# Attention weights transposed by a product with the diagonal of inverse denominators, in a pipeline one pair deeper, without the spreading products

## The chip, the cores and the metric

One core of a Trainium2 chip runs the whole kernel. The metric is the device time of one execution in microseconds (us), as a median over runs. "A product" below is one matrix product on TensorE (PE); in fp32 it leaves two records in the trace, a PE transpose leaves one.

## The reference

The kernel computes one step of a two-layer backbone on 128 context and 512 latent tokens (model width 1024). Each layer has adaLN-modulated RMSNorm, one input projection, three parallel head groups, an output projection and a SwiGLU FFN. The head group that matters here is the attention:

```python
def softmax_with_sink(s, sink):
    sk = sink.astype(jnp.float32).reshape(N_KV_HEADS, Q_PER_KV, 1, 1)
    m = jnp.maximum(jnp.max(s, axis=-1, keepdims=True), sk)
    e = jnp.exp(s - m)
    return e / (jnp.sum(e, axis=-1, keepdims=True) + jnp.exp(sk - m))

    # latent_attention: queries in blocks of 128, keys of the block before, the same and the next one
    s_lat = jnp.einsum('bnqkgd,bnskd->bnkgqs', qb, kband) * ATTN_SCALE
    s_ctx = jnp.einsum('bnqkgd,bckd->bnkgqc', qb, k_ctx.astype(jnp.float32)) * ATTN_SCALE
    s_lat = jnp.where(mask[None, :, None, None], s_lat, NEG)
    p = softmax_with_sink(jnp.concatenate([s_lat, s_ctx], axis=-1), sink)
    o = (jnp.einsum('bnkgqs,bnskd->bnqkgd', p[..., :3 * BLOCK], vband)
         + jnp.einsum('bnkgqc,bckd->bnqkgd', p[..., 3 * BLOCK:], v_ctx.astype(jnp.float32)))
```

There are 8 query heads and 2 key/value heads of 64 channels. The other two groups are RWKV-7 mixing (a chunked recurrence) and a Fourier transform; they and the FFN are not changed.

## The kernel before

Each engine has its own instruction stream, written by hand in one block per engine: `tensor` (PE), `scalar` (ACT), `vector` (DVE), `gpsimd` (POOL), `sync`. Semaphores order them; there is no scheduler, so each engine works strictly in the order of its stream. A layer runs: input projection, low-rank and Fourier products, attention stage A, two groups of the recurrence, attention stage B, three groups of the recurrence, output projection, FFN. So there are four attention stages in an execution.

A stage works through "pairs" m = (query block b, head j); a pair holds the two heads g = 0, 1 of the two key/value groups, one above the other in the 128 partitions. Stage A has 8 pairs (blocks 0 and 1), stage B 12 (blocks 2, 3 and the context block 4). Block 0 and 3 read 3 key tiles of 128, blocks 1 and 2 read 4, block 4 reads 1. For each pair:

- S, `scores(m)` on PE (the products of line 1332): queries times keys into PSUM, into two banks used in turn;
- softmax, `softmax_in(m)` on DVE: line 2447 writes the sink column, line 2449 adds the mask, takes the maximum and writes the scores into `Pm` (3 buffers) for each g;
- exp, `pexp(m)` on ACT (line 1940): exponentials in place and their sum into `den`;
- T, `transposes(m)` on PE (line 1355): each 128x128 tile of `Pm` through a PE transpose into PSUM bank 4 or 5 (one for each g, a single buffer);
- `ptcopy(m)` on ACT (line 1951): PSUM to `PT`;
- inverse, `inverse(m)` on DVE: reciprocal of `den` (line 2456), then `dg` = identity times 1/den, 128x2x128 (line 2459);
- V, `values(m)` on PE (line 1370): values times `PT`, summed over the key tiles, into columns 0 to 127 of bank 6 or 7; then the spreading products (line 1374), ones times `dg`, which put 1/den of each query into all rows of columns 128 to 255;
- `normalise(m)` on DVE: a copy of the spread inverses (line 2469), then the multiplication of the output with them (line 2470), into `qt`.

In iteration m of the loop PE does S(m), T(m-1), V(m-2); ACT does exp(m), ptcopy(m-1); DVE does softmax(m), normalise(m-3), inverse(m-1) and, in some iterations, a piece of other work (`between`). When the last S is done PE also transposes the first tiles of the next recurrence group (`token_tiles`, lines 1319 to 1322), and after the last V it runs that group's `products`. T(m) waits for exp(m) and for `pt_sb`, ptcopy of the pair before.

Ahead of stage A PE does `lora_rows("w", 1)`, a column step, `ada_rows(10)`, `lora_rows("a", 1)` (lines 977, 978), and then `ft1` (line 1242), and ACT does the matching `lora_sigmoid` (lines 1828, 1829) and row copies (line 1801). PE's step for ft1 needs the PSUM bank that the sigmoid of ("a", 1) reads.

Of the kernel before, what the change touches and what calls it, by code (L numbers as in the profile page):

```python
# [280 lines left out]
def build(nc, I, O):  # L281
# [5 lines left out]
    MUL, ADD, SUB, MAX = ALU.mult, ALU.add, ALU.subtract, ALU.max  # L287
    ctx = ExitStack()
    with ctx:
# [640 lines left out]
        def _(e):  # L930
# [33 lines left out]
            for l in range(DEPTH):  # L964
# [81 lines left out]
                def ada_cols(j, la):  # L1046

                    e.wait_ge(mrow_sb.sem, mrow_sb.upto(la, j + 1))
                    bank, at = (ps[4], 8 * ADA_BLOCK[j]) if j < 4 else (ps[5], 8 * j)
                    last = mm(bank[:, at:at + 8], mrow[:, :],  # L1050
                              ident.rearrange("p (g s) -> p g s", g=4)[:, :, 0:2], start=True, stop=True)
                    last.then_inc(mcol_ps(), 1)
# [212 lines left out]

                lora_rows("w", 1)
                ada_cols(9, l)
                ada_rows(10, l)
                lora_rows("a", 1)
                taken(e, l, ("fn", 0))  # L1270
                taken(e, l, ("fn", 1))
                e.wait_ge(ld_dft.sem, ld_dft.upto(l, ld_dft.per))
# [64 lines left out]
                def attention(first, last_pair, items_before, scored, then):  # L1337

                    def scores(m):
                        if m - 2 < first:  # L1340
                            q_ = (m + 1) % 2
                            e.wait_ge(acc_free[q_].sem, acc_free[q_].upto(l, (items_before + 1 - q_) // 2))
                        else:
                            e.wait_ge(s_sb.sem, s_sb.upto(l, 2 * (m - 1)))
                        score_products(m)

                    def transposes(m):
                        b, j = ATT[m]
                        for g in range(2):
                            n = 2 * m + g  # L1350
                            e.wait_ge(p_exp.sem, p_exp.upto(l, n + 1))
                            if n >= 2:
                                e.wait_ge(pt_sb.sem, pt_sb.upto(l, n - 1))
                            for c in range(len(key_tiles(b))):
                                last = tr(ps[4 + g][:, 128 * c:128 * c + 128], Pm[:, m % 3, g, 1 + 128 * c:129 + 128 * c],  # L1355
                                          ident)
                            last.then_inc(pt_ps(), 1)

                    def values(m):
                        b, j = ATT[m]  # L1360
                        bank = ps[6 + m % 2]
                        if m >= 2:
                            e.wait_ge(o_sb.sem, o_sb.upto(l, m - 1))
                        e.wait_ge(pt_sb.sem, pt_sb.upto(l, 2 * m + 2))
                        tiles = key_tiles(b)
                        for c, (kind, t) in enumerate(tiles):
                            for g in range(2):
                                v = (ckv[:, 1, 64 * g:64 * g + 64] if kind == "cache"
                                     else vtok[:, 128 * t + 64 * g:128 * t + 64 * g + 64])
                                mm(bank[64 * g:64 * g + 64, 0:128], v, PT[:, m % 4, c, g, :],  # L1370
                                   start=(c == 0), stop=(c == len(tiles) - 1))
                        e.wait_ge(den_diag.sem, den_diag.upto(l, m + 1))
                        for g in range(2):
                            last = mm(bank[64 * g:64 * g + 64, 128:256], ones[:, :], dg[:, m % 2, g, :],
                                      start=True, stop=True)
                        last.then_inc(pv_done(), 1)

                    for m in range(first, last_pair + 2):
                        if m < last_pair and m >= first + scored:
                            scores(m)  # L1380
                        if first <= m - 1 < last_pair:
                            transposes(m - 1)
                        if m == last_pair:
                            ready_for(then)
                            e.wait_ge(s_sb.sem, s_sb.upto(l, 2 * last_pair))
                            for n in range(2):
                                token_tiles(then, n)
                        if first <= m - 2 < last_pair:
                            values(m - 2)
                    for n in range(2):  # L1390
                        products(then, n)

# [327 lines left out]
        def _(e):  # L1720
# [36 lines left out]
            for l in range(DEPTH):  # L1757
# [40 lines left out]
                def ada_rows(j, la):  # L1798
                    e.wait_ge(ada_done.sem, ada_done.upto(la, 2 * j + 2))
                    e.wait_ge(mcol_ps.sem, mcol_ps.upto(la, j))  # L1800
                    act(mrow[:, :], ps[6 + j % 2][:, 0:128], ACT.Copy).then_inc(mrow_sb(), 1)
# [114 lines left out]
                act(kcT[:, :], cx[:, 256:384], ACT.Copy).then_inc(free(), 1)  # L1916
                ada_rows(9, l)
                lora_sigmoid("w", 1)
                ada_rows(10, l)
                lora_sigmoid("a", 1)  # L1920
                act(exp_table[:, :], eps[:, 0:1], ACT.Exp)
                ft1_copy(0)
                ft1_copy(1)
# [9 lines left out]
                def attention(first, last_pair):  # L1933

                    def pexp(m):
                        b, j = ATT[m]
                        w = 128 * len(key_tiles(b)) + 1
                        for g in range(2):
                            e.wait_ge(s_sb.sem, s_sb.upto(l, 2 * m + g + 1))
                            act(Pm[:, m % 3, g, 0:w], Pm[:, m % 3, g, 0:w], ACT.Exp, scale=-1.0,  # L1940
                                bias=negm[:, b % 2, j, g:g + 1],
                                accum_out=den[:, b % 2, j, g:g + 1]).then_inc(p_exp(), 1)

                    def ptcopy(m):
                        b, j = ATT[m]
                        nt = len(key_tiles(b))
                        if m >= 4:
                            e.wait_ge(pv_done.sem, pv_done.upto(l, m - 3))
                        for g in range(2):
                            e.wait_ge(pt_ps.sem, pt_ps.upto(l, 2 * m + g + 1))  # L1950
                            act(PT[:, m % 4, 0:nt, g, :], ps[4 + g][:, 0:128 * nt].rearrange("p (c t) -> p c t", c=nt),
                                ACT.Copy).then_inc(pt_sb(), 1)

                    for m in range(first, last_pair + 1):
                        if m < last_pair:
                            pexp(m)
                        if first <= m - 1 < last_pair:
                            ptcopy(m - 1)

                attention(0, NATT_A)  # L1960

# [232 lines left out]
        def _(e):  # L2194
# [77 lines left out]
            for l in range(DEPTH):  # L2272
# [165 lines left out]
                def attention(first, last_pair, between):  # L2438
# [14 lines left out]
                    def inverse(m):  # L2453
                        b, j = ATT[m]
                        e.wait_ge(p_exp.sem, p_exp.upto(l, 2 * m + 2))
                        own.after(V.reciprocal(den[:, b % 2, j, :], den[:, b % 2, j, :]))
                        if m >= 2:
                            e.wait_ge(pv_done.sem, pv_done.upto(l, m - 1))
                        V.tensor_tensor(dg[:, m % 2, :, :], ident.unsqueeze(1).to_broadcast([128, 2, 128]),
                                        den[:, b % 2, j, :].unsqueeze(2).to_broadcast([128, 2, 128]),  # L2460
                                        MUL).then_inc(den_diag(), 1)

                    def normalise(m):
                        b, j = ATT[m]
                        bank = ps[6 + m % 2]
                        e.wait_ge(pv_done.sem, pv_done.upto(l, m + 1))
                        if m >= 2:
                            e.wait_ge(o_sb.sem, o_sb.upto(l, m - 1))
                        own.after(V.tensor_copy(inv_row[:, m % 2, :], bank[:, 128:256]))
                        V.tensor_tensor(qt[:, j, 128 * b:128 * b + 128], bank[:, 0:128], inv_row[:, m % 2, :], MUL).then_inc(o_sb(), 1)  # L2470

                    for m in range(first, last_pair + 3):
                        if m < last_pair:
                            softmax_in(m)
                        if first <= m - 3 < last_pair:
                            normalise(m - 3)
                        if first <= m - 1 < last_pair:
                            inverse(m - 1)
                        if m - first in between:
                            kind, step = between[m - first]  # L2480
                            kind(step)
# [422 lines left out]
```

## Time and profile before

| what | us |
|---|---|
| median of 3 runs | 1833.74 (1831.01 to 1835.14) |
| the profiled execution | 1831.18 |
| its span, first to last instruction | 1829.2 |
| PE busy | 1741.3 (95%) |
| DVE busy | 1064.0 (58%) |
| ACT busy | 803.5 (44%) |
| mean granted TensorE clock | 0.994 |

Time in a trace counts from the first instruction. A timeline row is a run of instructions of one line on one engine: its start, its length, what it writes and reads, how many records; a bracket tells how long the engine sat idle before it and what ended that. Records on PE overlap (one lasts about 0.27 us, the next begins after 0.05 to 0.22 us), so costs on PE are read from start to start.

### The profile page before, as it was taken

What the parts mean: (1) busy time and instruction counts of PE and PEld (TensorE: products, weight loads), DVE (VectorE), ACT (ScalarE), POOL (GpSimd) and SP (SyncE); (2) the same over time, 40 slices, a digit from 0 to 9 for tenths busy, and PEclk for the clock granted to TensorE, in tenths of its full rate; (3) what the DMA queues carried; (4) which work ended last, traced back from release to release, by engine and by line L of the source; (5) the groups of instructions that cost most, each with busy time, mean ns of one, the idle gap of its engine ahead of it and who ended that gap; (6) DMA issues with size and microseconds to landing.
All of it is one profiled execution on the core that took longest, in us unless ns stands there. A gap on an engine that the chain in (4) does not pass through costs nothing. (4 is left out here: it accounts for less than half of the span.)

```text
span 1829.2 us, 46190 instructions
## 1 busy us (share of the span) xinstructions
PE 1741.3 (95%) x19693; PEld 1629.1 (89%) x19693; DVE 1064.0 (58%) x2328; ACT 803.5 (44%) x1729; POOL 370.7 (20%) x306
## 2 busy tenths in 40 slices
PE   7999988889999999999999999888999999999997
PEld 5999776779899999999989987677898999999997
DVE  4535767663494673838453556675619647365663
ACT  3343655552453351535443356465326525344352
POOL 3254010212302003020324431002231120201112
PEclk9999999999999999999999999999999999999999
DMA  9654600004613313241327362000021232323211
GB/s 335 212 128 143 170 5 3 4 6 130 172 58 88 86 60 102 59 114 53 99 88 202 92 195 64 4 3 7 25 70 51 65 107 68 104 61 90 84 56 58
DMA packets 215973, 161.11 MB, mean 88 GB/s; under 512 B 21968, under 2 KB 213146, under 8 KB 215770
## 3 DMA queue, kind: packets, MB, share of 16 engines
q1 hardware_dynamic: 213818, 156.13, 29.0%
q8 instruction: 157, 2.57, 0.6%
q0 software_dynamic: 1952, 2.03, 0.4%
q14 instruction: 46, 0.38, 0.1%
HBM read 154.99 MB, written 3.15 MB: 86 GB/s over the span
## 5 line engine op out<-in xcount | busy, mean ns | idle before, releaser
L2674 DVE SCALAR_TENSOR_TENSOR x<-PS,mod,x 128x320 f32<-128x320 f32 (+2 forms) x240 | 90.8, 434 | 289.3 <-PE PS L1082 289.3
L1118 PE MATMUL PS<-T_hi,wsplit 128*128 128x320 f32 x768 | 170.0, 309 | 0.0
L822 POOL TENSOR_TENSOR SfR<-ring,SfR 128x768 fp32r<-128x768 f32 (+1 forms) x24 | 41.2, 1715 | 582.3 <-ACT SfR L1790 582.3
L1081 PE MATMUL PS<-in_hi,win 128*128 128x320 f32 x480 | 149.9, 320 | 0.7 <-POOL win L822 0.7
L1082 PE MATMUL PS<-in_hi,win 128*128 128x320 f32 x480 | 144.6, 309 | 0.0
L1081 PE MATMUL PS<-hid_hi,wsplit 128*128 128x320 f32 x440 | 133.1, 310 | 0.0
L1082 PE MATMUL PS<-hid_hi,wsplit 128*128 128x320 f32 x440 | 132.5, 309 | 0.0
L1118 PEld LDWEIGHTS PS<-T_hi,wsplit 128*128 128x128 f32 x768 | 128.3, 188 | 0.0
L1118 PE MATMUL PS<-h_hi,wsplit 128*128 128x320 f32 x576 | 127.6, 309 | 0.0
L1118 PE MATMUL PS<-T_lo,wsplit 128*128 128x320 f32 x384 | 118.7, 309 | 0.0
L2107 ACT ACTIVATE wsplit<-Sf 128x512 fp32r<-128x512 f32 x96 | 59.8, 629 | 130.0 <-DVE Sf L2724 72.3
L2744 DVE TENSOR_TENSOR E<-E,PS 128x320 f32<-128x320 f32 x120 | 58.6, 488 | 87.4 <-PE PS L1118 87.1
L822 POOL TENSOR_TENSOR win<-ring,win 128x1024 fp32r<-128x1024 f32 x30 | 72.5, 2416 | 161.6 <-ACT win L1790 161.4
L1790 ACT ACTIVATE win<-ring 128x1024 fp32r<-128x1024 f32 x30 | 31.8, 1061 | 153.7 <-PE PS L1082 130.0
L822 POOL TENSOR_TENSOR wsplit<-ring,wsplit 128x768 fp32r<-128x768 f32 (+2 forms) x42 | 74.3, 1775 | 119.4 <-ACT wsplit L1790 119.4
L1118 PEld LDWEIGHTS PS<-h_hi,wsplit 128*128 128x128 f32 x576 | 96.3, 188 | 0.0
L1081 PEld LDWEIGHTS PS<-in_hi,win 128*128 128x128 f32 x480 | 90.0, 188 | 4.8 <-issue 4.2
L1082 PEld LDWEIGHTS PS<-in_hi,win 128*128 128x128 f32 x480 | 90.2, 188 | 1.9 <-issue 1.9
L1118 PE MATMUL PS<-h_lo,wsplit 128*128 128x320 f32 x288 | 89.0, 309 | 0.0
L886 POOL TENSOR_TENSOR mix<-mix,eye 128x128 f32<-128x128 f32 x40 | 16.5, 413 | 343.6 <-DVE mix L2521 343.6
L1081 PEld LDWEIGHTS PS<-hid_hi,wsplit 128*128 128x128 f32 x440 | 82.6, 188 | 0.5 <-issue 0.5
L1082 PEld LDWEIGHTS PS<-hid_hi,wsplit 128*128 128x128 f32 x440 | 82.6, 188 | 0.0
(539 smaller groups left out, 5399.4 us busy)
## 6 DMA issues: line engine op xcount, KB each, us to landing
ring<-in_w_ada SPq DMA_DIRECT2D x47, 1024.0 KB, 6.8
ring<-in_ffn_w_in SPq DMA_DIRECT2D x88, 512.0 KB, 5.1
ring<-in_ffn_w_out SPq DMA_DIRECT2D x16, 768.0 KB, 4.4
ring<-in_ffn_w_out SPq DMA_DIRECT2D x16, 640.0 KB, 4.0
ring<-in_w_in SPq DMA_DIRECT2D x7, 1024.0 KB, 9.6
ring<-in_w_in SPq DMA_DIRECT2D x10, 512.0 KB, 5.6
ring<-in_w_in SPq DMA_DIRECT2D x16, 256.0 KB, 5.6
ring<-in_w_out SPq DMA_DIRECT2D x16, 256.0 KB, 8.1
```

Source lines behind the costliest of these rows:

```text
L822: nc.gpsimd.tensor_tensor(lo, raw_w, hi, SUB).then_inc(wl_ready(), 1)
L886: nc.gpsimd.tensor_tensor(E1D[p], LP[p][:, :, BA, :], eye64[:, :].unsqueeze(1).to_broadcast([128, 2, 64]), ADD).then_inc(diag_sb(), 1)
L1081: mm(lat[:, 0:TH], w, v[:, 0:TH], start=(n == 0), stop=(n == total - 1))
L1082: last = mm(cx[:, 0:TH], w, v[:, TH:T], start=(n == 0), stop=(n == total - 1))
L1118: last = mm(bank[:, 0:TH], (w_lo if p == 1 else w_hi)[:, k, :], (v_lo if p == 2 else v_hi)[:, k, :], start=(q in (A11, A12, S1_) and k == ...
L1790: act(hi, raw_w, ACT.Copy).then_inc(wh_ready(), 1)
L2107: act(hi, raw_b, ACT.Copy).then_inc(bh_ready(), 1)
L2674: last = V.scalar_tensor_tensor(x[:, m, a:b], bank[:, at:at + b - a], mod[:, gate_at + m, s:s + 1], x[:, m, a:b], MUL, ADD)
L2744: V.tensor_tensor(v, v, bank[:, 0:TH], op).then_inc(ps_taken(), 1)
```

## The change

Four edits, in all three compute engines:

1. T multiplies each tile of `Pm` by `dg[:, m % 2, g, :]` in place of transposing it through the identity: the result is the transposed tile with each query's column already divided by its denominator. T waits for `den_diag` (the inverse of the pair) in place of `p_exp`.
2. The two spreading products of V are left out, and normalise is one copy of the output.
3. The pipeline is one pair deeper: in iteration m PE does S(m), T(m-2), V(m-3); ACT exp(m), ptcopy(m-2); DVE softmax(m), inverse(m-1), normalise(m-4). The token tiles now stand ahead of T(last-1). Each loop has one iteration more. `dg` is free for reuse once T has read it.
4. `lora_rows("a", 1)` on PE and `lora_sigmoid("a", 1)` on ACT stand ahead of `ada_rows(10)`.

```diff
@@ PE, ahead of the Fourier transform
                 lora_rows("w", 1)
                 ada_cols(9, l)
+                lora_rows("a", 1)
                 ada_rows(10, l)
-                lora_rows("a", 1)
@@ PE, attention
                     def transposes(m):
                         b, j = ATT[m]
+                        e.wait_ge(den_diag.sem, den_diag.upto(l, m + 1))
                         for g in range(2):
                             n = 2 * m + g
-                            e.wait_ge(p_exp.sem, p_exp.upto(l, n + 1))
                             if n >= 2:
                                 e.wait_ge(pt_sb.sem, pt_sb.upto(l, n - 1))
                             for c in range(len(key_tiles(b))):
-                                last = tr(ps[4 + g][:, 128 * c:128 * c + 128], Pm[:, m % 3, g, 1 + 128 * c:129 + 128 * c],
-                                          ident)
+                                last = mm(ps[4 + g][:, 128 * c:128 * c + 128], Pm[:, m % 3, g, 1 + 128 * c:129 + 128 * c],
+                                          dg[:, m % 2, g, :], start=True, stop=True)
                             last.then_inc(pt_ps(), 1)
@@ PE, values(m)
-                                mm(bank[64 * g:64 * g + 64, 0:128], v, PT[:, m % 4, c, g, :],
-                                   start=(c == 0), stop=(c == len(tiles) - 1))
-                        e.wait_ge(den_diag.sem, den_diag.upto(l, m + 1))
-                        for g in range(2):
-                            last = mm(bank[64 * g:64 * g + 64, 128:256], ones[:, :], dg[:, m % 2, g, :],
-                                      start=True, stop=True)
+                                last = mm(bank[64 * g:64 * g + 64, 0:128], v, PT[:, m % 4, c, g, :],
+                                          start=(c == 0), stop=(c == len(tiles) - 1))
                         last.then_inc(pv_done(), 1)
 
-                    for m in range(first, last_pair + 2):
+                    for m in range(first, last_pair + 3):
                         if m < last_pair and m >= first + scored:
                             scores(m)
-                        if first <= m - 1 < last_pair:
-                            transposes(m - 1)
                         if m == last_pair:
                             ready_for(then)
                             e.wait_ge(s_sb.sem, s_sb.upto(l, 2 * last_pair))
                             for n in range(2):
                                 token_tiles(then, n)
                         if first <= m - 2 < last_pair:
-                            values(m - 2)
+                            transposes(m - 2)
+                        if first <= m - 3 < last_pair:
+                            values(m - 3)
@@ ACT
                 lora_sigmoid("w", 1)
+                lora_sigmoid("a", 1)
                 ada_rows(10, l)
-                lora_sigmoid("a", 1)
@@ ACT, attention
-                    for m in range(first, last_pair + 1):
+                    for m in range(first, last_pair + 2):
                         if m < last_pair:
                             pexp(m)
-                        if first <= m - 1 < last_pair:
-                            ptcopy(m - 1)
+                        if first <= m - 2 < last_pair:
+                            ptcopy(m - 2)
@@ DVE, inverse(m) and normalise(m)
                         if m >= 2:
-                            e.wait_ge(pv_done.sem, pv_done.upto(l, m - 1))
+                            e.wait_ge(pt_ps.sem, pt_ps.upto(l, 2 * (m - 1)))
@@
-                        own.after(V.tensor_copy(inv_row[:, m % 2, :], bank[:, 128:256]))
-                        V.tensor_tensor(qt[:, j, 128 * b:128 * b + 128], bank[:, 0:128], inv_row[:, m % 2, :], MUL).then_inc(o_sb(), 1)
-
-                    for m in range(first, last_pair + 3):
+                        V.tensor_copy(qt[:, j, 128 * b:128 * b + 128], bank[:, 0:128]).then_inc(o_sb(), 1)
+
+                    for m in range(first, last_pair + 4):
                         if m < last_pair:
                             softmax_in(m)
-                        if first <= m - 3 < last_pair:
-                            normalise(m - 3)
                         if first <= m - 1 < last_pair:
                             inverse(m - 1)
+                        if first <= m - 4 < last_pair:
+                            normalise(m - 4)
```

## Rows read from the trace of the kernel before

**Rows 1.** The page: busy time of engines, share, instructions.

```profile
PE 1741.3 (95%) x19693; PEld 1629.1 (89%) x19693; DVE 1064.0 (58%) x2328; ACT 803.5 (44%) x1729; POOL 370.7 (20%) x306
```

**Rows 2.** First stages A and B: stretch, length, busy PE, PEld, DVE, ACT, POOL, clock, DMA.

```profile
210.76:238.51 27.75, 25.46 (x273) 20.00 (x272) 20.39 (x74) 21.55 (x57) 0.00 (x0) 1.00 0.20 66
292.52:326.50 33.98, 31.13 (x328) 23.26 (x328) 27.99 (x112) 24.29 (x75) 0.00 (x0) 1.00 0.01 2
```

**Rows 3.** Timeline of PE in the first stage A: start, length, line, tiles, records.

```profile
218.27 0.88 PE L1355 MATMUL PS<-mats,mix 128*128 128x128 f32 x6
219.08 0.66 PE L1370 MATMUL PS<-mix 128*64 128x128 f32 x8
219.57 0.39 PE L1370 MATMUL PS<-mix,ckv 128*64 128x128 f32 x4
219.79 0.39 PE L1374 MATMUL PS<-mix,ones 128*64 128x128 f32 x4
220.10 0.92 PE L1332 MATMUL PS<-mix 64*128 64x384 f32 x4
...
221.17 0.88 PE L1355 MATMUL PS<-mats,mix 128*128 128x128 f32 x6
...
231.06 1.09 PE L1355 MATMUL PS<-mats,mix 128*128 128x128 f32 x8
232.08 0.88 PE L1370 MATMUL PS<-mix 128*64 128x128 f32 x12
```

**Rows 4.** PE's lines 1355 and 1374 in the whole execution (ns min/median/max).

```profile
L1355 PE MATMUL PS<-mats,mix x240: 272/273/331, 213.3 to 1216.0; 128*128 128x128 f32 x120
L1374 PE MATMUL PS<-mix,ones x160: 270/271/273, 217.1 to 1218.1; 128*64 128x128 f32 x160
```

**Rows 5.** Timeline of PE: single fp32 products of 128x128, last steps before stage A.

```profile
210.10 0.38 PE L1262 MATMUL PS<-mix 128*128 128x128 f32 x2
210.32 0.39 PE L1263 MATMUL PS<-mix 128*128 128x128 f32 x2
210.54 0.29 PE L1050 MATMUL PS<-mats,mrow 128*128 128x8 f32 x2
```

**Rows 6.** The weight loads of line 1262 (ns min/median/max).

```profile
L1262 PEld LDWEIGHTS PS<-mix x8: 187/188/188, 205.6 to 1102.7; 128*128 128x128 f32 x8
```

**Rows 7.** PE's waits in the first stages A and B (us, times, longest).

```profile
PE PS L1355 <- ACT mix L1951: 1.4, 3, 0.9
PE PS L1355 <- ACT mix L1940: 0.7, 1, 0.7
...
PE PS L1355 <- ACT mix L1951: 1.8, 5, 0.6
PE PS L1355 <- ACT mix L1940: 1.0, 1, 1.0
```

**Rows 8.** Timeline of DVE at the opening of stage A.

```profile
214.30 0.43 DVE L2459 TENSOR_TENSOR mix<-mats,den 128x256 f32<-128x256 f32 x1
```

**Rows 9.** Timeline of DVE and PE at the opening of stage B, and at its fifth pair.

```profile
296.79 0.43 DVE L2459 TENSOR_TENSOR mix<-mats,den 128x256 f32<-128x256 f32 x1
...
303.82 0.49 PE L1332 MATMUL PS<-kcT,mix 64*128 64x128 f32 x4
```

**Rows 10.** Timeline of ACT and PE ahead of stage A: the low-rank and Fourier steps.

```profile
194.39 0.28 ACT L1801 ACTIVATE mrow<-PS 128x128 f32<-128x128 f32 x1 [0.46 <-PE PS L1041]
...
192.37 1.95 PE L1041 MATMUL PS<-ring,csil 128*32 128x128 f32 x64
194.25 1.14 PE L977 MATMUL PS<-mix,lora 64*128 64x512 f32 x4
...
196.84 0.67 PE L1242 MATMUL PS<-mix 128*128 128x256 f32 x2 [1.23 <-ACT mix L1829]
```

**Rows 11.** Timeline of DVE: normalise of one pair.

```profile
219.61 0.29 DVE L2469 COPY mix<-PS 128x128 f32<-128x128 f32 x1
...
220.15 0.15 DVE L2456 RECIPROCAL den<-den 128x2 f32<-128x2 f32 x1
```

## The prediction

> **What bounds the kernel now.** The first view to read is the busy time of the engines: PE is busy for 1741.3 of 1829.2 us, DVE for 1064.0, ACT for 803.5 [rows 1]. That says that PE bounds most of the execution, not that it bounds the attention, so I read the four attention stages by themselves. In the first layer they last 27.75 and 33.98 us, of which PE is busy for 25.46 and 31.13, 5.1 us of idle time in all; the second-busiest engine of stage A, ACT, has 21.55 of 27.75, and that of stage B, DVE, 27.99 of 33.98 [rows 2]. The second layer runs the same code on the same shapes, so one stage A and one stage B carry the argument, and each counts twice. The clock granted in both is 1.00, the 2.4 GHz level.
>
> Then PE's timeline, from start to start. For a pair of 3 key tiles T takes 219.08 - 218.27 = 0.81 us, V 219.79 - 219.08 = 0.71, the spreading products 220.10 - 219.79 = 0.31, and S of the following pair, with 4 tiles, 221.17 - 220.10 = 1.07 [rows 3]. Start follows start there with no idle time, so in the middle of a stage PE sets the pace. What idle time there is stands at the opening, where the first T waits for the first exponentials, and in front of some T, which wait for ACT's copy (line 1951) of the pair before: 0.7 + 1.4 us in stage A and 1.0 + 1.8 in stage B are named [rows 7]. The stages thus hold work to be added to (PE's) and some 5 us a layer of named waits that could take it up.
>
> **The transposing products.** A T of 3 tiles has 6 records in 0.81 us, one of 4 tiles 8 records in 232.08 - 231.06 = 1.02 [rows 3]. Two more records make 0.21, so a transpose costs 0.11 us and each T a fixed 0.15 or so (0.81 - 6 x 0.11). There are 240 of them in the execution [rows 4]. What replaces each is a full fp32 product, 128 rows, 128 stationary and 128 moving columns, with a new stationary tile each time. The trace has that form in lines 1262 and 1263: 210.32 - 210.10 = 0.22 and 210.54 - 210.32 = 0.22 us [rows 5]. Its two weight loads last 0.188 us each [rows 6], and 0.22 is less than two of them, so they lie beside the products. Added: 240 x (0.22 - 0.11) = +26.4 us of PE work. The form is the same, but at most two stand in a row there, with six or eight to come; the bounds are 0.11 (no dearer than the transpose) and 0.376 (both weight loads bare, 2 x 0.188). I take 0.22, because it is the same shape on the same engine.
>
> The row shows a product at twice the price of a transpose. The Trainium skill, "TensorE: Matmul & The Clock Gate", section Terms, says that transpose mode is 4 times faster for FP32, and "Perfetto Trace Analysis", section Transposes, asks that a logical transpose be done as a transpose and not as a matmul. By the first the price would be 4 x 0.11 = 0.44 and the term 240 x 0.33 = +79 us; by the rows it is +26.4. The second speaks against this edit, and the rows agree with its direction.
>
> **The spreading products.** Of the 0.31 us between 219.79 and the next S about 0.09 is the gap that follows V in any case: the four records before them, of the same form, take only 219.79 - 219.57 = 0.22 [rows 3]. There are 160 records, four for each of 40 pairs [rows 4]: 40 x 0.22 = -8.8 us. On DVE normalise lasts from 219.61 to 220.15, 0.54 us, and becomes one copy of about 0.25 [rows 11]: -0.3 us a pair on an engine that PE's work covers. Worth nothing, unless DVE is what T waits for.
>
> PE's work so grows by 26.4 - 8.8 = +17.6 us, or for stage A (56 products, 8 pairs) 6.2 - 1.8 = +4.4, for stage B (64 products, 12 pairs) 7.0 - 2.6 = +4.4.
>
> **The deeper pipeline, stage A.** The chain that ended the waits in the middle of a stage is S(m-1), softmax(m-1), exp(m-1), ptcopy of an earlier pair, T. It has the same links after the change: T(m-2) needs the bank that ptcopy(m-3) frees, and that stands on ACT behind exp(m-1). But between the end of S(m-1) and this T lie a T, a V and an S of PE, 1.02 + 8 x 0.11 = 1.90, then about 1.02 and 1.07, together 3.99 us for 4 tiles where it was 1.02 + 1.24 + 1.07 = 3.33. The waits that were left over in the middle go; the new wait for the diagonal is a pair old by then and is met. At the opening there is more waiting: T(0) now stands behind S(2), which cannot start before softmax(0), and needs the diagonal of pair 0, which DVE has ready at 214.30 + 0.43 = 214.73 [rows 8]; before, T(0) waited 0.7 us for exp(0) and no more [rows 7]. What is queued behind this wait on PE is S(3), T(1), V(0), and ACT and DVE wait for these. From there: T(0) 0.81 + 0.66 = 1.47, S(3) 0.86, T(1) after a wait for ACT of about 0.2 us (exp(2) stands ahead of ptcopy(0)) 1.47, V(0) 0.8: S(4) starts near 219.5, against 220.10 [rows 3]. But then T and V are each a pair behind. Left are: S 4 x 1.07, T 2 x 1.47 + 4 x 1.90, V 3 x 0.8 + 4 x 1.02, and the token tiles, about 1: 22.3 us. The last V ends near 241.7, against 238.51 [rows 2]: **+3.2 us**, of PE's +4.4.
>
> **Stage B.** The same steps: the diagonal of its first pair is ready at 296.79 + 0.43 = 297.22; then T 1.90, S 1.07, T 1.90, V 1.02, and S(12), the fifth, starts near 303.2, against 303.82 [rows 9]. Left are S 4 x 0.86 + 4 x 0.42, T 2 x 1.90 + 4 x 1.47 + 4 x 0.6, V 3 x 1.02 + 4 x 0.8 + 4 x 0.4, the tokens 1: 26.1 us, to 329.3. After the last, short V the products of the recurrence wait for ACT, whose two token copies now come behind the last ptcopy: 0.3. So 329.5, against 326.50 [rows 2]: **+3.0 us**. Two layers: 2 x (3.2 + 3.0) = +12.4. The one bound is all of the +17.6 (nothing taken up), the other all of the waits of [rows 7] taken up, 17.6 - 2 x 4.9 = +7.8, and with the unnamed idle time too (2 x 5.1 [rows 2]) +7.4.
>
> **The order ahead of the stage.** PE waits 1.23 us for the sigmoid of ("a", 1), from 195.6 to 196.84 [rows 10]. After the change the ("a", 1) products stand ahead of the row step, which hides that sigmoid; but they use the banks of ("w", 1) and wait for its sigmoids, of which the second ended at 194.39 - 0.46 = 193.93. The second product of ("a", 1) takes half of 195.61 - 194.25 = 1.36, to 194.6, and the row step 194.25 - 192.37 = 1.88, so ft1 starts at about 196.6 [rows 10]: -0.2 us a layer; most of the wait only moves (bounds 0 and -1.2). ACT's row copy comes behind four sigmoids now, and its readers come later still. Sum: 12.4 - 0.4 = **+12.0 us**.
>
> Nothing else moves: the recurrence that follows waits for PE's token tiles and products, and the weight transfers have no part in the stages (DMA share 0.01 in B [rows 2]).
>
> **The rivals.** First, *the weight loads lie bare in a row of products* (or the skill's ratio holds): 0.376 a product, 240 x 0.27 = +64, less 8.8 and the waits: some +50 to +70, 1884 to 1904 us. For it: loads of 0.188 us [rows 6] against passes of 0.11. Against it: 0.22 from start to start in [rows 5]. Second, *DVE's diagonal becomes the gate*: each T waits for reciprocal and diagonal (0.6 us) beyond what it waited for; if the extra pair of depth did not cover it, 36 x 0.6 = +22 more, 1867 us. Against it: DVE is busy for 3 to 5 us less than PE in a stage [rows 2], and loses 0.3 a pair. Third, *not slower*: PE's step in the row of products is less than in [rows 5], since part of the 0.15 fixed us at each T is load time that a longer product hides, and the deeper pipeline takes up all waits. At 0.11 + 0.06 = 0.17 us a product, 240 x 0.06 - 8.8 = +5.6, less the 9.8 of waits and 0.4: -4.6 us, 1829 us; from about 0.19 down with all waits gone the change is not slower. For it: only that one row has this form; against it: two starts in it, both 0.22, and the opening waits that grow. Last, *the extra depth does nothing*: the waits stay, +17.2, 1851 us, inside the range.
>
> **How the numbers follow.** The profiled execution took 1831.2 us, 2.0 more than its span, so 1831.2 + 12.0 = 1843.2; the median of the runs is 2.6 us above that execution, 1833.7, which gives 1845.7. I state 1845.0. Chances: forecast with its bounds (+6 to +19) 0.82; bare loads 0.04; DVE as the gate 0.04; not slower 0.10, of which 0.06 lie within 0.2% (3.7 us, about what a measurement of this kernel can tell from no change) and 0.04 below. The range goes from 1837 (+5.5 from 1831.5, a little past all waits taken up) to 1854 (+18 to +20, no wait taken up and products of 0.23).
>
> **What would show it.** In the changed kernel line 1355 has 480 records with starts 0.11 apart, line 1374 is gone, T of 3 tiles lasts 1.47 and of 4 tiles 1.90 from start to start; PE is idle at each opening for over 1 us behind DVE's diagonal and hardly later; the stages last about 31.0 and 37.0 us; ft1's wait of 1.23 shrinks while one at the products of ("a", 1) appears. A step other than 0.22 for a product, or waits of T for line 2459 in the middle of a stage, would make the prediction wrong.

## The result and the profile after

The changed kernel takes 1848.24 us in the median of 4 runs (1846.32 to 1849.97), the kernel before 1832.57 us on the same chips (1831.01 to 1835.14): a ratio of 1.0082 with a 95% interval of 1.0070 to 1.0095. It is 0.8% slower. The profiled execution of it took 1847.58 us, its span is 1845.6 us, 16.4 us more than the span before.

The page of the changed kernel, sections 1 and 4 (busy time of the engines; shares of the chain that ended last by line):

```profile
PE 1760.0 (95%) x19773; PEld 1651.9 (90%) x19773; DVE 1051.3 (57%) x2288; ACT 804.5 (44%) x1729; POOL 370.8 (20%) x306
...
PE PS L1118 13%; PE PS L1081 9%; PE PS L1082 9%; PE PS L1355 2%; PE PS L1041 1%; PE PS L1370 1%; PE PS L1332 1%; PE PS L977 1%; DVE mix L2516 0%; PE PS L961 0%; ACT h_hi L1747 0%; ACT mix L2003 0%; ACT h L2071 0%; PE PS L1605 0%; DVE h_lo L2257 0%
```

PE is busy for 18.7 us more than in [rows 1], DVE for 12.7 us less, and line 1355, the transposing products, is now the fourth line of the chain. Busy time by stretch of the changed kernel, the first stages A and B (stretch, length, busy PE, PEld, DVE, ACT, POOL, clock, DMA):

```profile
211.62:242.84 31.22, 29.96 (x297) 25.41 (x296) 18.38 (x67) 20.62 (x54) 0.00 (x0) 1.00 0.18 60
294.89:332.29 37.40, 35.69 (x345) 28.90 (x345) 25.37 (x102) 23.69 (x74) 0.00 (x0) 1.00 0.01 2
```

Its waits of PE in stage A, and behind the dots in stage B (us, times, longest):

```profile
PE PS L1355 <- DVE mix L2455: 0.8, 1, 0.8
PE PS L1332 <- DVE negm L2445: 0.5, 1, 0.5
...
PE PS L1355 <- DVE mix L2455: 0.8, 1, 0.8
PE PS L1332 <- DVE negm L2445: 0.8, 1, 0.8
```

Against [rows 2], stage A is 3.47 us longer and stage B 3.41; in the second layer the same stages are 3.46 and 3.33 us longer: 13.7 of the 16.4 us. Against [rows 7], no T waits for ACT's copy any more (line 1947 here); what is left stands at the opening, at S(2), which waits for DVE's maximum of pair 0 (`negm`), and at T(0), which waits for the diagonal (line 2455). PE is idle for 1.26 us of stage A and 1.71 of stage B, where it was 2.29 and 2.85 [rows 2]. The timeline of PE in the changed kernel, opening and steady part of stage A:

```profile
213.97 0.70 PE L1332 MATMUL PS<-mix 64*128 64x256 f32 x4 [0.47 <-DVE negm L2445]
214.50 0.39 PE L1332 MATMUL PS<-kcT,mix 64*128 64x128 f32 x4
215.65 1.60 PE L1355 MATMUL PS<-mix 128*128 128x128 f32 x12 [0.76 <-DVE mix L2455]
217.19 0.70 PE L1332 MATMUL PS<-mix 64*128 64x256 f32 x4
...
224.85 1.60 PE L1355 MATMUL PS<-mix 128*128 128x128 f32 x12
226.39 0.66 PE L1370 MATMUL PS<-mix 128*64 128x128 f32 x8
226.88 0.39 PE L1370 MATMUL PS<-mix,ckv 128*64 128x128 f32 x4
227.19 0.92 PE L1332 MATMUL PS<-mix 64*128 64x384 f32 x4
227.94 0.39 PE L1332 MATMUL PS<-kcT,mix 64*128 64x128 f32 x4
228.26 2.05 PE L1355 MATMUL PS<-mix 128*128 128x128 f32 x16
230.24 0.66 PE L1370 MATMUL PS<-mix 128*64 128x128 f32 x8
```

T of 3 tiles has 12 records from 224.85 to 226.39, 1.54 us (0.81 before); T of 4 tiles 16 records from 228.26 to 230.24, 1.98 us (1.02 before [rows 3]). Two more products cost 0.44, so one costs 0.22 and each T a fixed 0.2 or so. V and the gap behind it last 227.19 - 226.39 = 0.80, where they lasted 1.02. Start follows start: in the steady part PE sets the pace, with more to do.

### The profile page after: what moved, and what is told of

Its sections match the earlier page's. It is cut to its first block and busy times, and to the rows that moved or that the text cites. A ratio compares the mean times of both kernels' runs of the same rounds, so it can differ in the third digit from the quotient of the medians.

```text
span 1845.6 us, 46274 instructions
## 1 busy us (share of the span) xinstructions
PE 1760.0 (95%) x19773; PEld 1651.9 (90%) x19773; DVE 1051.3 (57%) x2288; ACT 804.5 (44%) x1729; POOL 370.8 (20%) x306
## 5 line engine op out<-in xcount | busy, mean ns | idle before, releaser
L886 POOL TENSOR_TENSOR mix<-mix,eye 128x128 f32<-128x128 f32 x40 | 16.4, 411 | 358.8 <-DVE mix L2516 358.8
```

## The experiments

The stages below are read from the first record of S to the first record of the recurrence's `products`, in the trace of each kernel, in us. The ratio is to the kernel before, with its 95% interval. A stage in which the granted clock was under 0.98 has it in brackets; all the others had 0.99 or more.

| kernel | ratio | A, B (layer 1) | A, B (layer 2) |
|---|---|---|---|
| before | 1 | 27.75, 33.99 | 27.75, 34.35 |
| changed | 1.0082 (1.0070 to 1.0095) | 31.22, 37.40 | 31.21, 37.68 |
| e5, product with the identity | 1.0114 (1.0099 to 1.0129) | 32.38, 39.60 | 32.38, 39.87 |
| e6, no spreading products | 0.9992 (0.9982 to 1.0001) | 26.33, 32.17 | 26.33, 32.48 |
| e3, depth alone | 0.9996 (0.9987 to 1.0006) | 27.73, 34.20 | 27.71, 34.19 |
| e4, changed at the old depth | 1.0641 (1.0623 to 1.0659) | 54.77 (0.81), 65.50 (0.84) | 49.88 (0.90), 71.15 (0.74) |
| e1, changed with the old order | 1.0075 (1.0057 to 1.0093) | 31.22, 37.38 | 31.21, 39.28 (0.96) |
| e8, weights scaled on DVE | 1.0007 (0.9997 to 1.0017) | 26.94, 34.59 (0.95) | 26.93, 33.83 (0.95) |
| e9, as e8, copy first on ACT | 0.9989 (0.9979 to 0.9999) | 25.99, 32.53 | 25.98, 32.52 |
| e10, before, deeper, copy first | 0.9945 (0.9926 to 0.9963) | 25.43, 31.46 | 25.42, 31.45 |
| e12, as e1, copy first | 1.0064 (1.0041 to 1.0087) | 31.22, 38.99 (0.96) | 31.20, 37.38 |

The theory was that the product costs twice a transpose and that this decides the sign; the rivals were a product with its weight loads bare (nothing running beside them), DVE's diagonal as the gate, and waits large enough to take everything up.

**The product by itself** (e5):

```diff
-                                last = tr(ps[4 + g][:, 128 * c:128 * c + 128], Pm[...], ident)
+                                last = mm(ps[4 + g][:, 128 * c:128 * c + 128], Pm[...], ident, start=True, stop=True)
```

> The kernel before with one edit: each of the 240 transposes of line 1355 is a full fp32 product with the identity in place of a PE transpose; depth, spreading products and order stay. Output unchanged. Theory (a product takes 0.22 to 0.23 us from start to start, a transpose 0.11, and the waits in front of T in the middle of a stage take up a part): T of 3 tiles 1.5 us, of 4 tiles 1.98 us from start to start; PE work +27 us, of which the four stages take up about 2 us each; about +20 us on the kernel before. Rival 1, weight loads bare: 0.376 us a product, +55 us or more. Rival 2, nothing is taken up: +27 us.

Median 1850.86 us, 1830.73 before: +20.1. The weight loads and the products of line 1355, all instructions of that line (least, median and largest ns):

```profile
L1355 PEld LDWEIGHTS PS<-mats,mix x480: 186/192/192, 214.4 to 1235.3; 128*128 128x128 f32 x160
L1355 PE MATMUL PS<-mats,mix x480: 275/275/377, 214.4 to 1235.5; 128*128 128x128 f32 x160
```

PE's waits in its stages A and, behind the first dots, B of layer 1:

```profile
PE PS L1355 <- ACT mix L1940: 0.7, 1, 0.7
...
PE PS L1355 <- ACT mix L1940: 1.0, 1, 1.0
...
PE PS L1355 <- ACT mix L1951: 0.4, 1, 0.4
```

The loads last 0.19 us each, two for a product that costs 0.22: they stay beside the products even in a row of 16 records, so the rival of bare loads falls. The waits for line 1951 have gone from 1.4 and 1.8 us [rows 7] to none and 0.4, with the old depth. PE's longer T covers them by itself, without a deeper pipeline. The theory holds, in size too.

**Without the spreading products** (e6; the output is not divided):

```diff
-                        e.wait_ge(den_diag.sem, den_diag.upto(l, m + 1))
-                        for g in range(2):
-                            last = mm(bank[64 * g:64 * g + 64, 128:256], ones[:, :], dg[:, m % 2, g, :], ...)
```

> The kernel before without the two spreading products of each pair and with normalise as one copy of the output, so the attention's output is not divided by the denominators. Theory 1 (PE's work sets the pace, 0.22 us a pair): -8.8 us. Theory 2 (at the old depth the chain S, softmax, exp, copy, T is nearly as long as PE's work of a pair, so what is taken from PE turns into waits of T for line 1951): the named waits of T grow by 1 us a stage, and the time falls by 4 to 6 us only.

The stages give back 1.42, 1.82, 1.42 and 1.87, 6.5 us in all, of 8.8 us of PE work taken away; the waits of T for the copy (line 1947 here) grow from 1.4 and 1.8 us to:

```profile
PE PS L1355 <- ACT mix L1947: 1.8, 4, 1.1
...
PE PS L1355 <- ACT mix L1947: 2.4, 6, 0.6
```

So a part turned into waits, as theory 2 has it, though they grew by 0.4 and 0.6 us and not by 1. The time as a whole fell by 1.5 us only, not by 4 to 6, with an interval that takes in no change. The trace cannot settle that difference: it is of the fastest of the ten executions, 1826.07 us against a median of 1829.21. In it the two recurrences between A and B are 1.2 and 1.1 us longer than in the kernel before; what such differences are is the matter of the last experiment.

**The depth alone** (e3): before with `transposes(m - 2)`, `values(m - 3)`, `ptcopy(m - 2)`, `normalise(m - 4)` and the loops of the change; `dg` with three buffers.

> The kernel before with the pipeline one pair deeper and nothing else (PE transposes and spreading products stay; the diagonal gets a third buffer so that no new wait arises). Theory (the added PE work of the change had its cover from the deeper pipeline only in part, since that removes the waits in the middle and adds some at the opening): stage A -0.5 to -1.5 us, stage B -1 to -2 us, -4 to -6 us in all. Rival (depth changes nothing by itself, because T waits for the same copy behind the same exponentials): within 1 us of the kernel before.

Nothing: 1830.34 us against 1830.73. The theory fell here, and the trace of e3 shows how. PE at the opening of its stage A:

```profile
212.96 0.87 PE L1355 MATMUL PS<-mats,mix 128*128 128x128 f32 x6
213.77 0.70 PE L1332 MATMUL PS<-mix 64*128 64x256 f32 x4
...
216.20 0.90 PE L1355 MATMUL PS<-mats,mix 128*128 128x128 f32 x6 [1.51 <-ACT mix L1951]
```

And ACT in the same stretch:

```profile
214.38 0.62 ACT L1940 ACTIVATE mix<-mix,negm 128x385 f32<-128x385 f32 x1 [0.32 <-DVE negm L2449]
...
215.00 0.60 ACT L1940 ACTIVATE mix<-mix,negm 128x385 f32<-128x385 f32 x1
...
215.59 0.84 ACT L1951 ACTIVATE mix<-PS 128x384 f32<-128x384 f32 x2
```

T(0) is done by 213.8, but its copy out of the single PSUM buffer starts at 215.59, since it stands on ACT behind exp(2), which waits for softmax(2). T(1) needs that buffer and waits 1.51 us. The waits for line 1951 are 1.9 us in stage A, 1.5 of them here: most of what stood in the middle has only moved to the second T.

**Copy first** (e10): e3, and on ACT

```diff
-                        if m < last_pair:
-                            pexp(m)
                         if first <= m - 2 < last_pair:
                             ptcopy(m - 2)
+                        if m < last_pair:
+                            pexp(m)
```

> The kernel before, one pair deeper (as e3_depth_only), and in each iteration ACT does ptcopy(m-2) ahead of exp(m). Output as before. Theory (deepening changed nothing because it moved the wait for ACT's copy from the middle to the second T, where the copy stands behind exp(2)): that wait of 1.5 us goes, stage A 26.2, stage B 32.5 us, about 6 us less than the kernel before. Rival (the depth itself is without effect): within 1 us of e3_depth_only.

Median 1821.54 us, 1831.96 before: 10.4 us faster. PE's waits in its stages A and, behind the dots, B of layer 1:

```profile
PE PS L1332 <- DVE negm L2449: 0.5, 1, 0.5
...
PE PS L1332 <- DVE negm L2449: 0.8, 1, 0.8
```

The two stretches:

```profile
212.02:237.45 25.43, 24.93 (x273) 20.07 (x272) 20.21 (x74) 20.62 (x54) 0.00 (x0) 1.00 0.22 72
290.24:321.70 31.46, 30.51 (x329) 23.14 (x329) 28.06 (x113) 23.83 (x74) 0.00 (x0) 1.00 0.01 2
```

No T waits for anything. PE is busy for 24.93 of 25.43 us of stage A, where it was 25.46 of 27.75 [rows 2]. The theory holds, but the expected size was too small: 10.1 us in the four stages (2.32, 2.53, 2.33, 2.90), not 6. Depth alone is worth nothing (e3); with the copy first it gives the one kernel here that is clearly faster than the kernel before. The copy first at the old depth was not tried, so whether the 10 us need both is not shown.

**The old depth with the new product** (e4): the changed kernel with `transposes(m - 1)`, `values(m - 2)`, `ptcopy(m - 1)`, `normalise(m - 3)`.

> The changed kernel at the depth of before: PE does S(m), T(m-1), V(m-2), ACT exp(m), ptcopy(m-1), DVE softmax(m), inverse(m-1), normalise(m-3). Theory (without the extra pair T waits for the diagonal, which DVE makes behind softmax(m)): each T waits about 2.2 us for line 2455 at 4 tiles and 1.9 at 3, the period of a 4-tile pair is 6.3 us in place of 3.9; about +75 us on the changed kernel, 1920 us. Rival (the depth does nothing, the diagonal is ready anyway): 1848 us as the changed kernel, T waits for line 2455 under 0.3 us.

Median 1948.16 us: 100 us above the changed kernel. PE's timeline, in stage A:

```profile
235.74 2.14 PE L1355 MATMUL PS<-mix 128*128 128x128 f32 x12 [2.22 <-DVE mix L2455]
...
243.03 3.42 PE L1355 MATMUL PS<-mix 128*128 128x128 f32 x16 [2.25 <-DVE mix L2455]
...
250.75 2.05 PE L1355 MATMUL PS<-mix 128*128 128x128 f32 x16 [2.21 <-DVE mix L2455]
```

And the whole stretch:

```profile
211.72:266.49 54.77, 39.88 (x298) 33.09 (x297) 18.45 (x67) 22.90 (x55) 0.00 (x0) 0.81 0.10 34
```

Seven T wait for the diagonal for 1.9 to 2.25 us each, as expected, 14.9 us in stage A. The rival, that the depth does nothing, falls: with this product the extra pair is what keeps DVE's diagonal off the path. The stage got 23.5 us longer, though. PE's idle time accounts for 13.6 of them, its busy time, 39.88 for 29.96, for 9.9, and that is the clock: for a part of the stage PE ran at the 1.2 GHz level. The T of 4 tiles at 243.03 took 3.34 us to the next line with 0.56 granted, the one at 250.75 took 1.99 with 1.00. The clock fell for the first time in T(0) (0.58 granted), behind the stage's first idle stretch of 2.15 us, and after that PE was idle for about 2 us of every 6 to 8. Over the four stages 64.4 us are idle time of PE and 39.4 its longer busy time at the lower clock, where 75 us of waits alone were expected.

**The same gain with the changed product?** (e12): e1 with the copy first.

> The changed kernel with its fourth edit undone (as e1_after_old_order), and ACT doing ptcopy(m-2) ahead of exp(m). Theory (with the transposing products PE's own work sets the pace everywhere but at the opening, so the copy has slack in any case): the stages stay within 0.3 us of 31.2 and 37.4 us, the time within 2 us of e1_after_old_order, 1845 us. That would leave the product's price as what parts this kernel from e10_depth_copy_first. Rival (the copy order is worth its 10 us here too): 1836 us.

1844.94 us, 1845.54 for e1: no gain, as the theory says. Stage A is 31.22 with either order. Its first stage B is longer, 38.99, with a granted clock of 0.96, the same as in the second B of e1; at a clock of 1.00 both have 37.38. With both stages B at 37.38 its four stages are 23.4 us longer than those of e10. The work of the products less that of the spreading products is 17.6 of them and the longer fixed part of T (below) 2.7; the remaining 3.1 are PE's idle time, 1.26 for 0.50 us in stage A and 1.70 for 0.95 in B, which is the wait of T(0) for the diagonal. So the product brings that wait too, and not only its price.

**Scaling on DVE** (e8, and e9 with the copy first):

```diff
-                        V.tensor_tensor(dg[...], ident..., den..., MUL).then_inc(den_diag(), 1)
+                        for g in range(2):
+                            last = V.tensor_scalar(Pm[:, m % 3, g, 1:w + 1], Pm[:, m % 3, g, 1:w + 1],
+                                                   den[:, b % 2, j, g:g + 1], None, MUL)
+                        last.then_inc(den_diag(), 1)
```

> The changed kernel, fourth edit undone, with a different way to divide: DVE multiplies the weights in place by 1/den, two instructions of 128 by 128 to 512 a pair, in place of making the diagonal, and PE transposes them with PE transposes again (0.11 us a tile for 0.225). The spreading products stay out, the depth is that of the change. Theory (the products with the diagonal are all that made the change slower, and PE's work is now 8.8 us less than before): the stages last 26.3 to 27 and 32 to 33 us, about 4 to 7 us in all less than before in the stages, 1826 us. Rival (the chain through ACT, exp(m-1) ahead of ptcopy, sets the pace once PE has less to do, as it did without the spreading products at the old depth, and the scaling makes the opening longer): 1830 us or no change.

> The kernel of e8_scaled_deep with one more edit: in each iteration ACT does ptcopy(m-2) ahead of exp(m). Theory (what T waits for in the middle and at the second T of a stage is the copy that stands behind exp on ACT; with the pair of depth the exponentials have slack and the copy has none): the waits of T for ACT's copy fall under 0.5 us a stage, stage A 25 to 25.8 us, stage B 30 to 31.5 us, and 10 us less than before in all, 1821 us. Rival (the wait only goes to the exponentials or to DVE): as e8_scaled_deep.

1833.44 us for e8 (1831.96 before), in the time its rival's answer: T waits 1.6 us for the copy and 1.1 for DVE in stage A. Its stages B do not show this cleanly, since both ran at a granted clock of 0.95: PE is busy in them for 29.97 us, in e9 with the same work for 28.17, so an estimated 1.8 us of each is the clock. In e9 the waits for the copy are gone, and a part of what it was to gain went to DVE. The waits in its stages A and, behind the dots, B:

```profile
PE PS L1355 <- DVE mix L2455: 2.0, 3, 1.1
...
PE PS L1355 <- DVE mix L2455: 3.1, 4, 1.3
```

One of them in the middle, in PE's timeline:

```profile
226.06 0.39 PE L1332 MATMUL PS<-kcT,mix 64*128 64x128 f32 x4
227.09 1.09 PE L1355 MATMUL PS<-mats,mix 128*128 128x128 f32 x8 [0.65 <-DVE mix L2455]
```

PE has 4.4 us less to do in a layer than in e10 and takes 1.6 us longer for the two stages: the scaling (0.75 to 0.88 us a pair on DVE) comes ahead of T, the division by the spread inverses comes behind V, where nobody waits. 1828.97 us is a gain of 2 to 3 us, where 10 were expected. That miss has two parts. In the stages e9 gains 6.8 us on the kernel before, where e10 gains 10.1; the other 4 us or so are lost outside the stages, and no run here says why.

**The order ahead of the stage** (e1): the changed kernel with its fourth edit undone.

> The changed kernel with its fourth edit undone: the low-rank products and sigmoids of (a, 1) stand behind the row step again. In the traces the stretch from the last products of the fifth projection to the attention is 0.3 us a layer longer after the change than before. Theory (the new order moves PE's wait from ft1 to the products of (a, 1), which now stand in two pieces, and gains nothing): this stretch is 0.3 us a layer shorter than in the changed kernel, the four attention stages as in the changed kernel (31.2 and 37.4 us); in all within 1 us of the changed kernel, 1846 to 1848 us. Rival (the order is worth what the forecast said, 0.2 us a layer gained): ft1 starts later here.

From the same product to ft1 the changed kernel takes 11.68 us, e1 11.39, and so does the kernel before. Medians: 1845.54 and 1848.24 (before beside them: 1831.96 and 1832.57), so 0.6 us of stretch is shown by the traces and the rest is within the spread; the stretch is as the theory has it, the medians are 2.7 us apart and not within 1. PE in the changed kernel:

```profile
193.69 1.53 PE L977 MATMUL PS<-mix,lora 64*128 64x512 f32 x3 [0.70 <-ACT mix L1825]
194.65 0.38 PE L978 MATMUL PS<-mix,lora 64*128 64x128 f32 x2
195.06 0.59 PE L977 MATMUL PS<-mix,lora 64*128 64x512 f32 x1
195.48 0.38 PE L978 MATMUL PS<-mix,lora 64*128 64x128 f32 x2
195.79 1.95 PE L1041 MATMUL PS<-ring,csil 128*32 128x128 f32 x64
```

**Code and stops** (e11, e13, e14): before with 32 waits that are already met on PE near the start; before again; changed again.

> The kernel before with 32 more instructions on PE, waits that are already met, in an idle stretch near the start; nothing else. Theory (the stops of PE in the recurrence that end in issue, and with them 1 to 3 us of the stretch between the attention stages, hang on where the instructions stand in PE's stream): the stages last 27.75 and 34.0 us as before, but the stops stand at other lines of the recurrence, and the stretches between the stages differ by over 0.5 us from 54.01 and 52.81. Rival (they hang on the moment, not the code): their places differ as much between this and before as between two executions of the same kernel.

> The kernel before, unchanged, profiled again. If the stops in issue hang on the code alone, they stand at the same lines and the stretches between the attention stages last 54.0 and 52.8 us again; if not, they differ by up to 2 us, and the 2 to 3 us that the changed kernel lost outside the attention are not its own.

> The changed kernel, unchanged, profiled again. The stages should last 31.2 and 37.4 us again within 0.1 us. The stretches between them 52.05 and 53.28 us if the stops hang on the code, up to 2 us off if they do not.

In their one execution each they took 1829.16, 1830.39 and 1846.04 us. The stages repeat within 0.03 us (27.75 and 33.98; 31.21 and 37.38). The recurrence between the first A and B does not: 54.01 and 54.46 in two executions of before, 51.42 in the padded one, 52.05 and 50.92 in two of the changed kernel. The stops of PE in it, in the kernel before:

```profile
250.19 0.39 PE L1516 MATMUL PS<-mix 64*64 64x192 f32 x4 [0.65 <-issue]
...
254.99 0.45 PE L1538 MATMUL PS<-mix 64*64 64x128 f32 x8 [1.37 <-issue]
...
276.35 0.33 PE L1499 MATMUL PS<-mix 64*64 64x64 f32 x2 [1.09 <-issue]
...
280.82 0.28 PE L1526 MATMUL PS<-mix 64*64 64x64 f32 x3 [0.83 <-issue]
```

The same in before again:

```profile
250.04 0.39 PE L1516 MATMUL PS<-mix 64*64 64x192 f32 x4 [0.38 <-issue]
...
255.40 0.45 PE L1538 MATMUL PS<-mix 64*64 64x128 f32 x8 [1.92 <-issue]
...
276.94 0.33 PE L1499 MATMUL PS<-mix 64*64 64x64 f32 x2 [1.37 <-issue]
...
281.40 0.28 PE L1526 MATMUL PS<-mix 64*64 64x64 f32 x3 [0.82 <-issue]
```

The same four lines stop in both; such stops add up to 3.9 and 4.5 us in this recurrence, and to 0.3 in the padded kernel. e3 and e10, whose PE stream has the same instructions in another order, stop at line 1538 as well, for 2.1 and 1.6 us; e5, with 240 more records in the stages, does not. So for the kernel before the theory holds: where the long stops stand hangs on where the instructions stand in PE's stream, their length on the moment. For the changed kernel it holds less well: its first recurrence differs by 1.1 us between two executions, and a stop in the second layer (line 1576) lasts 0.5 us in one of them and 0.2 in the other. What PE waits for in these stops, no view of the profile says.

## Why the prediction was right, and where it was off

Forecast were +12.0 us, slower, 1845.0 in a range of 1837 to 1854; measured 1848.24, +15.7 on the median of before. The sign and most of the size came from the right cause, the price of the product. Of the 4.4 us by which the span grew beyond the 12.0, 1.3 lie in the stages, 1.0 in the order ahead and 2.1 outside both. By its steps:

- **PE sets the pace in the middle of a stage.** Right. Stage A starts S(4) 220.38 - 211.62 = 8.76 us after its first S, forecast 8.7; it ends after 31.22, forecast 30.9.
- **0.22 us a product, +26.4 us.** Right: 0.22 in the changed kernel and in e5, which gives the edit alone +20.1 us. The two bounds and the rival of bare loads (0.376) are out. By the Trainium skill, "TensorE: Matmul & The Clock Gate", section Terms, transpose mode is 4 times faster for FP32; these runs show 0.22 against 0.11, twice, and the measurement decides. The Trainium skill, "Perfetto Trace Analysis", section Transposes, asks for transposes in place of matmuls, and e5 agrees, with 20.1 us.
- **The fixed part of T.** Mis-sized: the prediction carried over 0.15 to 0.17 us, and it is 0.2 to 0.22 (1.54 for 1.47, 1.98 for 1.90, 0.64 for 0.60). Over the pairs of a layer that is 8 x 0.07 + 8 x 0.08 + 4 x 0.04 = 1.4 us, 2.7 in all; some of it is returned elsewhere, and the stages came out 1.3 us above the 12.4.
- **The spreading products, -8.8 us.** Right in work (V 1.02 to 0.80), and e6 shows that it gives 6.5 us in the stages where the old pipeline cannot use the rest.
- **The deeper pipeline takes the waits of the middle and adds some at the opening.** The balance was right for the changed kernel: T(0) starts 4.03 us behind the first S, forecast 3.97. The cause was half right, and in that part the sum came out by luck: the prediction gave the depth the credit, but by e5 the longer T takes the waits at the old depth as well, and by e3 depth alone is worth nothing. What the depth does in this change is to cover DVE's diagonal, which the prediction named as a rival if it failed, at +22 us. By e4 the price without cover is 100 us: the prediction had 0.6 us a T, but the wait is 2.2, since the diagonal stands on DVE behind the softmax of the next pair, and the clock falls too.
- **The order ahead, -0.4 us.** Wrong in sign: +0.29 us a layer, +0.6. The step that failed is that the second product of ("a", 1) takes half of 1.36, 0.68 us: in the changed kernel it took 1.27, from 194.52, when its first record starts, to the row step at 195.79. The two products of ("a", 1) use half of the array's rows each. Back to back, their four large records took from 194.25 ([rows 10]) to the next line in PE's timeline of the kernel before:

```profile
195.21 0.40 PE L978 MATMUL PS<-mix,lora 64*128 64x128 f32 x4
```

  That is 0.96 us; apart, waiting for one sigmoid each, two records take 194.65 - 193.69 = 0.96 alone. The wait became shorter (1.23 to 0.70 us), and the pair lost its overlap. The starts of the single records bear this out: 194.25, 194.26, 194.78, 194.80 before, two by two, and 193.69, 194.22, 194.52, 195.06 in the changed kernel. No experiment tried it by itself.
- **Nothing else moves.** Nearly: 13.7 in the stages and 0.6 for the order leave 2.1 of 16.4 us. The recurrences differ by -1.96 and +0.47 us, the start of the kernel by +0.57, and the long stretches behind B by +1.35 and +1.76. e11, e13 and e14 show differences of 0.4 to 3 us in such stretches from a shift of the code or from one execution to the next, so these traces do not show them as a price of the edits, nor rule it out. How the 2.1 us divide stays open.
- **Not slower** (chance 0.10) is out: all waits of [rows 7] are gone, others of 1.3 and 1.6 us stand at the openings in their place, and the time is up by 15.7 us. e10 shows what those waits were worth with cheap transposes: 10.4 us, about the 10 us of idle time in [rows 2].

## What to carry to other kernels

In these runs a transpose in fp32 costs half a product, so folding a scale into it pays only if it saves more behind it than it adds for each tile: here it adds 240 x 0.11 us and saves 40 x 0.22. Before a pipeline is made deeper, ask what stands ahead of the late step on its own engine: here one pair more was worth nothing while the copy out of the only PSUM buffer stood behind an exponential on ACT, and 10 us once it stood ahead. And here a term that feeds the critical step early (scaling ahead of T, e9) cost the stages 3.3 us more than the same division where nobody waits for it (behind V, e10), although it left PE less to do.

## What the runs showed of the hardware

- The clock fell where PE was kept idle again and again: granted 0.74 to 0.90 over the stages of e4, with about 2 us of idle time in front of nearly every T. A T of 4 tiles took 1.99 us at 1.00 and 3.34 at 0.56. It also fell in a stage B that had no such waits (0.96 in one of two stages of e1 and of e12, 37.38 us to 39.28 and 38.99; 0.95 in both of e8), which cost 1.6 to 1.9 us a time. Why there, no run shows.
- Two products on 64 rows each ran side by side when issued back to back: four records of 512 columns in 0.96 us. Split by a wait, two of them took 0.96.
- PE stops in dense rows of 64x64 products for 0.4 to 1.9 us with nothing to wait for that the profile shows. In the kernel before the places repeat from one execution to the next, and they moved when 32 instructions were put ahead. The first recurrence lasted 51.4 us with the padding and 54.0 to 54.5 without: an accident of 2.6 to 3.0 us, nearly a fifth of what this change did.
